# Late modulation sums along rows, with transposed weights, and two steps of a projection group moved to the end of the chunk before

## What is computed

```python
def _modulation(cond, w_mod, b_mod):
    m = jax.nn.silu(cond) @ w_mod + b_mod
    return jnp.split(m, 3, axis=-1)          # shift, scale, gain

sh, sc, g = _modulation(c, w_mod[l], b_mod[l])           # latent tokens
shc, scc, gc = _modulation(c_ctx, w_mod[l], b_mod[l])    # context tokens
h = x * (1.0 + sc) + sh
q, k, v, z = jnp.split(h @ w_in[l], 4, axis=-1)
y = mixer(q, k, v)      # layer 0: neighbourhood attention, layer 1: differential attention
out = (y * jax.nn.silu(z)) @ w_out[l]
x = _layer_norm(DEEPNORM_ALPHA * x + (1.0 + g) * out, ln_g[l], ln_b[l])
```

## Time and profile before

| | |
|---|---|
| median of 3 runs | 1850.34 us (1850.16 to 1850.41) |
| profiled execution | 1850.39 us, span 1848.6 us |
| first layer, chunks 0 to 7 | about 64 to 842 us of the span |
| late loads | 64 DMAs of 256 KB, 2.7 us to landing in the median |
| granted clock of PE | 0.999 of full |

### The profile page before, as it was taken

How to read it: one execution, slowest core, us unless ns; L and a number is a source line. 1 busy time by engine, 2 the same in 40 slices (tenths; PEclk the granted TensorE clock), 3 DMA queues, 4 the chain that set the end, 5 groups by cost and what they waited for, 6 DMA issues and landing times. The chain is left out here.

```text
span 1848.6 us, 30835 instructions
## 1 busy us (share of the span) xinstructions
PE 1802.8 (98%) x10621; PEld 1554.1 (84%) x10621; DVE 1291.5 (70%) x2061; ACT 928.0 (50%) x1680; POOL 269.4 (15%) x219
## 2 busy tenths in 40 slices
PE   7999999999999999989999999999999999999998
PEld 3888888888888888878878889888888888898886
DVE  6677777778687877765868485675848484757658
ACT  2555555555555555560046555464736464554500
POOL 3100000000000000255431010101000010102951
PEclk9999999999999999999999999999999999999999
DMA  9512121312122222225420010101010100101343
GB/s 348 135 47 83 47 82 47 84 38 79 54 74 60 74 60 62 73 94 187 159 80 24 12 45 11 45 0 45 11 45 11 34 23 11 45 11 45 99 143 125
DMA packets 82111, 127.28 MB, mean 69 GB/s; under 512 B 49760, under 2 KB 49920, under 8 KB 81936
## 3 DMA queue, kind: packets, MB, share of 16 engines
q1 hardware_dynamic: 76048, 108.54, 18.7%
q0 software_dynamic: 2384, 8.39, 1.6%
q10 hardware_dynamic: 3632, 9.73, 1.3%
HBM read 108.90 MB, written 20.09 MB: 70 GB/s over the span
## 5 line engine op out<-in xcount | busy, mean ns | idle before, releaser
L548 PE MATMUL acc<-h_hi,w_hi 128*128 128x512 f32 (+1 forms) x1408 | 524.9, 373 | 3.1 <-DVE h_lo L473 1.6
L548 PE MATMUL acc<-h_hi,w_lo 128*128 128x512 f32 (+1 forms) x1408 | 508.7, 361 | 0.0
L548 PE MATMUL acc<-h_lo,w_hi 128*128 128x512 f32 (+1 forms) x1408 | 507.9, 361 | 0.0
L548 PEld LDWEIGHTS acc<-h_hi,w_lo 128*128 128x128 f32 x1408 | 265.3, 188 | 41.5
L548 PEld LDWEIGHTS acc<-h_hi,w_hi 128*128 128x128 f32 x1408 | 265.8, 189 | 40.3 <-DVE h_lo L473 4.7
L548 PEld LDWEIGHTS acc<-h_lo,w_hi 128*128 128x128 f32 x1408 | 266.3, 189 | 33.9
L1676 DVE TENSOR_REDUCE stats<-acc 128x1 f32<-128x1280 f32 x128 | 189.7, 1487 | 43.3 <-PE acc L1775 42.7
L1586 ACT ACTIVATE far_prob<-acc,stats 128x1280 f32<-128x1280 f32 x128 | 170.2, 1330 | 28.3 <-DVE stats L1676 26.5
L1593 ACT ACTIVATE far_pt<-acc 128x512 f32<-128x512 f32 (+1 forms) x192 | 101.1, 527 | 162.0 <-PE acc L1784 158.6
L1775 PE MATMUL acc<-k_dup,q_stack 128*128 128x512 f32 (+1 forms) x768 | 176.7, 367 | 1.8 <-ACT far_prob L1586 0.4
L1797 PE MATMUL acc<-far_pt,far_v 128*128 128x128 f32 x1280 | 172.7, 275 | 0.0
(11 more groups left out here) (208 smaller groups left out, 2906.8 us busy)
## 6 DMA issues: line engine op xcount, KB each, us to landing
w_raw<-in_w_in SPq DMA_DIRECT2D x64, 512.0 KB, 3.3
near_late_slots<-in_w_mod SPq DMA_DIRECT2D x64, 256.0 KB, 2.7
w_raw<-in_w_out SPq DMA_DIRECT2D x16, 512.0 KB, 3.2
w_raw<-y_t POOLq DMA_DIRECT2D x14, 448.0 KB, 5.0
y_t<-y SPq DMA_DIRECT2D x7, 640.0 KB, 3.1
modulation_rows<-in_w_scale SPq DMA_DIRECT2D x8, 512.0 KB, 6.9
modulation_rows<-in_w_mod SPq DMA_DIRECT2D x8, 512.0 KB, 6.7
out_rows<-in_x SPq DMA_DIRECT2D x8, 512.0 KB, 4.5
```

The source lines that it names most:

```text
L548: mm = nc.tensor.matmul(m.bank(self.bank_of(j, c), w), wt[:, b % 2, k, :], ht[:, k, t0:t0 + w], start=(k == 0 and i == 0), stop=(k == KT - ...
```

## The change

The late weights are transposed on the host (`w_late`), so that output columns are the partitions, and the sum over the 1024 inputs goes along a row: in two halves of 512, times four blocks of 128 columns, which are again eight loads of 128 x 512 (u = 4 x half + block). `sum` becomes, for each condition, one `tensor_tensor_reduce` of the slot with a row of coefficients (the condition, the same in all partitions), which writes one number per partition; the second half starts from the first half's number. `reduce` becomes `turn`, one transpose of the 128 x 8 sums. The unused product goes to a free probability buffer, to the slot itself, or, for u > 4, to the other slot; so loads 6 and 7, and the next chunk's load 0, wait for one sum more. The condition is turned at the start and stored in DRAM (`store_cond`); `load_coef` loads 512 of its columns, both conditions, to all partitions, once per half.

Places: SP issues load 6 no longer ahead of `load_next(6)` but behind the bias tables, together with load 7; `load_coef` of the second half stands ahead of load 5, that of the next chunk's first half behind the next chunk's load 1. In the last chunk loads 6 and 7 go behind `out_w.load` 2 and 4, sum 5 to the projections, sums 6 and 7 to DVE's steps 3 and 4, and the products of loads 6 and 7 go. The row is stored by two DMAs of 4 x 128.

Two of eight steps k of the next chunk's group 4 (`BEGUN = 2`) go from the projections to step 10, ahead of `turn`; for chunk 0 they go ahead of the loop. In the last chunk the output projection's pieces (4, 6) and (6, 7) become (4, 5), (5, 6) and (6, 7), the last in step 10.

```diff
+    def store_cond(self, sp):
+        sp.wait_ge(self.act, 2)
+        sp.dma_start(self.cond_rows.rearrange("c (k p) -> (c k) p", p=P), self.cond_buf).then_inc(self.cond_stored, 16)
+
+    def take_cond(self, act):
+        act.wait_ge(self.coef_ready, 1)
+        self.nc.scalar.activation(self.cond_buf, self.m.psum[0:2 * KT, 0, 0:P], ACT.Copy).then_inc(self.act, 1)
...
+        nc.tensor.transpose(m.psum[0:2 * KT, 0, 0:P], m.cond_act[:, :, :].rearrange("p c k -> p (c k)"), m.ident[:, :])\
+            .then_inc(self.coef_ready, 1)
...
     def load(self, sp, c, u):
         if u >= 2:
-            sp.wait_ge(self.summed, CREDIT + c * 2 * KT + 2 * (u - 1))
-        k = u % KT
-        src = self.w_mod[k * P:(k + 1) * P, bass.ds(c * 512 + (D + u // KT * 512), 512)]
-        sp.dma_start(self.slots[k % 2], src).then_inc(self.loaded[k % 2], 16)
+            sp.wait_ge(self.summed, CREDIT + c * 2 * KT + 2 * (u if 5 < u <= KT else u - 1))
+        half = u % KT // 4
+        src = self.w_late[bass.ds(c * 512 + (u // KT * 512 + u % 4 * P), P), half * 512:(half + 1) * 512]
+        sp.dma_start(self.slots[u % 2], src).then_inc(self.loaded[u % 2], 16)
+
+    def load_coef(self, sp, c, half):
+
+        sp.wait_ge(self.summed, CREDIT + c * 2 * KT + KT * half)
+        first = self.cond_rows[0, half % 2 * 512:half % 2 * 512 + 1]
+        src = bass.AP(first.tensor, first.offset, [[0, P], [D, 2], [1, 512]])
+        sp.dma_start(self.coef, src).then_inc(self.coef_loaded, 16)
 
     def sum(self, v, c, u):
+
+        half, t = u // 4, u % 4
         v.wait_ge(self.loaded[u % 2], CREDIT + c * 8 * KT + 16 * (u // 2 + 1))
+        if t == 0:
+            v.wait_ge(self.coef_loaded, CREDIT + c * 32 + 16 * (half + 1))
         if u == 0:
-            v.wait_ge(self.reduced, CREDIT + c * 1)
+            v.wait_ge(self.turned, CREDIT + c * 1)
+        v.wait_ge(self.summed, CREDIT + c * 2 * KT + 2 * u)
+        x = self.slots[u % 2]
         for cnd in range(2):
-            x, coef = self.slots[u % 2], self.m.cond_act[:, cnd, u:u + 1]
-            if u == 0:
-                ins = self.nc.vector.tensor_scalar(self.acc[cnd], x, coef, None, ALU.mult)
-            else:
-                if cnd == 0:
-                    v.wait_ge(self.summed, CREDIT + c * 2 * KT + 2 * u)
-                ins = self.nc.vector.scalar_tensor_tensor(self.acc[cnd], x, coef, self.acc[cnd], ALU.mult, ALU.add)
-            ins.then_inc(self.summed, 1)
-
-    def reduce(self, pe, c, bank):
+            col = cnd * 4 + t
+            unused = x if cnd else self.slots[1 - u % 2] if u > 4 else self.unused[u % 2]
+            self.nc.vector.tensor_tensor_reduce(out=unused, in0=x, in1=self.coef[:, cnd, :], scale=0.5,
+                                                scalar=self.sums[:, 0, col:col + 1] if half else 0.0, op0=ALU.mult, op1=ALU.add,
+                                                accum_out=self.sums[:, half, col:col + 1]).then_inc(self.summed, 1)
+
+    def turn(self, pe, c, bank):
 
         pe.wait_ge(self.summed, CREDIT + c * 2 * KT + 2 * KT)
-        for cnd in range(2):
-            mm = self.nc.tensor.matmul(self.m.psum[0:2, bank, :], self.m.pick[:, cnd, :], self.acc[cnd],
-                                       start=(cnd == 0), stop=(cnd == 1))
-        mm.then_inc(self.reduced, 1)
-
-    def reduce_last(self, pe, c, bank):
-
-        for u in (KT - 2, KT - 1):
-            pe.wait_ge(self.loaded[u % 2], CREDIT + c * 8 * KT + 16 * (u // 2 + 1))
-            self.nc.tensor.matmul(self.m.psum[0:2, bank, :], self.m.cond_act[:, :, u], self.slots[u % 2],
-                                  start=(u == KT - 2), stop=False)
-        pe.wait_ge(self.summed, CREDIT + c * 2 * KT + 2 * (KT - 2))
-        for cnd in range(2):
-            mm = self.nc.tensor.matmul(self.m.psum[0:2, bank, :], self.m.pick[:, cnd, :], self.acc[cnd],
-                                       start=False, stop=(cnd == 1))
-        mm.then_inc(self.reduced, 1)
+        self.nc.tensor.transpose(self.m.psum[0:8, bank, 0:P], self.sums[:, 1, :], self.m.ident[:, :]).then_inc(self.turned, 1)
 
     def take_row(self, act, c, bank):
-        act.wait_ge(self.row_stored, CREDIT + c * 16)
-        act.wait_ge(self.reduced, CREDIT + c * 1 + 1)
-        self.nc.scalar.activation(self.row, self.m.psum[0:2, bank, :], ACT.Copy, scale=0.5).then_inc(self.row_ready, 1)
+        act.wait_ge(self.row_stored, CREDIT + c * 32)
+        act.wait_ge(self.turned, CREDIT + c * 1 + 1)
+        self.nc.scalar.activation(self.row, self.m.psum[0:8, bank, 0:P], ACT.Copy).then_inc(self.row_ready, 1)
 
     def store_row(self, sp, c):
         sp.wait_ge(self.row_ready, CREDIT + c * 1 + 1)
-        sp.dma_start(self.mod_rows[:, bass.ds(c * 512 + ROW_PAD, 512)], self.row).then_inc(self.row_stored, 16)
+        for cnd in range(2):
+            sp.dma_start(self.mod_rows[cnd, bass.ds(c * 4 + ROW_PAD // P, 4), :], self.row[4 * cnd:4 * cnd + 4, :]).then_inc(self.row_stored, 16)
...
-        self.product(pe, c, 4)
+        self.product_part(pe, c, 4, self.BEGUN, KT)
...
-        if not last:
+        if last:
+            late.sum(v, c, 5)
+        else:
             self.split_lo_part(v, self.nc.vector, c, 4)
...
+    fill[NU, MIDDLE] = (1, 4, 0, p.BEGUN)
     filled = {step: piece[0:2] for (step, half), piece in fill.items() if piece[3] == KT}
-    fill_last = {(5, MIDDLE): (0, 2), (7, MIDDLE): (2, 4), (9, MIDDLE): (4, 6), (9, END): (6, 7)}
+    fill_last = {(5, MIDDLE): (0, 2), (7, MIDDLE): (2, 4), (9, MIDDLE): (4, 5), (9, END): (5, 6), (NU, MIDDLE): (6, 7)}
...
-                    for u in (3, 4, 5, 6):
+                    for u in (3, 4):
                         late.load(sp, c, u)
+                    late.load_coef(sp, c, 1)
+                    late.load(sp, c, 5)
                     if last:
                         for k in range(KT):
                             out_w.load(sp, p, k)
-                            if k == 3:
-                                late.load(sp, c, 7)
+                            if k in (2, 4):
+                                late.load(sp, c, 6 if k == 2 else 7)
                     else:
                         p.load_next(sp, c, (6,))
                         biases[1].wait(sp)
...
-                        for u in (7, KT, KT + 1):
+                        for u in (6, 7, KT, KT + 1):
                             late.load(sp, c, u)
+                        late.load_coef(sp, c, 2)
                     late.store_row(sp, c)
...
+                modulation.store_cond(sp)
                 load_first(sp)
...
+                modulation.take_cond(act)
                 p.split_hi_part(act, 0, 0)
...
-                        if col == 0:
-                            act.wait_ge(late.row_stored, CREDIT + c * 16)
...
-                        if step == 3 and last:
-                            late.sum(v, c, 5)
+                        if last and step in (3, 4):
+                            late.sum(v, c, step + 3)
...
+                p.product_part(pe, 0, 4, 0, p.BEGUN)
...
-                                late.reduce_last(pe, c, 1)
-                            else:
-                                late.reduce(pe, c, 7)
+                            late.turn(pe, c, 1 if last else 7)
...
+    w_late = a(np.concatenate([w_mod[0, :, 2 * D:], w_mod[1]], axis=1).T)
```

More of the change, by code:

```diff
@@ L237, in activate @@
         act.wait_ge(self.small_in, 48)
-        self.nc.scalar.activation(self.m.cond_act[:, :, :], self.m.cond[:, :, :], ACT.Tanh, scale=0.5).then_inc(self.tanh_done, 1)
+        self.nc.scalar.activation(self.m.cond_act[:, :, :], self.m.cond[:, :, :], ACT.Tanh, scale=0.5).then_inc(self.act, 1)
     def exp_lambda(self, act):
         act.wait_ge(self.dve, 2)
-        self.nc.scalar.activation(self.sums[:, 2:4], self.sums[:, 0:2], ACT.Exp).then_inc(self.lam_exp, 1)
+        self.nc.scalar.activation(self.sums[:, 2:4], self.sums[:, 0:2], ACT.Exp).then_inc(self.act, 1)
     def take_rows(self, act):
@@ L255, in scale_part @@
         nc.vector.memset(m.mean_mat[:, :], 1.0 / P)
-        for r in range(2):
-            nc.vector.memset(m.pick[:, r, r:r + 1], 1.0)
-            nc.vector.memset(m.pick[:, r, 1 - r:2 - r], 0.0)
         for t in range(KT):
@@ L368, with __init__ @@
     AHEAD = 2
-    def __init__(self, nc, m, near, stack, w_mod, mod_rows):
-        self.nc, self.m, self.w_mod, self.mod_rows = nc, m, w_mod, mod_rows
+    def __init__(self, nc, m, near, stack, w_late, cond_rows, mod_rows):
+        self.nc, self.m, self.w_late, self.cond_rows, self.mod_rows = nc, m, w_late, cond_rows, mod_rows
         sem = lambda n: stack.enter_context(nc.semaphore("x_" + n))
         self.slots = [near.late_slots[:, i, :] for i in range(2)]
-        self.acc = [near.late_acc[:, i, :] for i in range(2)]
-        self.row = near.late_row
+        self.coef, self.row, self.sums = near.late_coef, near.late_row, near.late_sums
+        self.unused = [near.prob[:, 2 + i, 0:512] for i in range(2)]
@@ L597 @@
```

(5 more changed lines are left out.)

53 lines of the change are left out of this document (30 added, 23 removed).

## The result

| | kernel before | changed kernel |
|---|---|---|
| median | 1850.25 us (1850.14 to 1850.41, 4 runs) | 1873.02 us (1871.45 to 1873.70, 4 runs) |
| profiled execution | 1850.39 us, span 1848.6 us | 1873.32 us, span 1871.4 us |
| PE's granted clock, mean | 0.999 | 0.990 (0.990 to 0.992 in the four runs) |

The change costs 1.2%: the ratio is 1.0121, with a 95% interval of 1.0108 to 1.0133. The direction is the predicted one, but the time lies 13 us above the forecast of 1859.6 and outside its range.

A forecast was written before the change was run, and what follows sets the result against it. TensorE (PE), 98% busy, was taken as the bound. 7 x (1.00 + 0.3) per loop chunk, -0.3 for the last chunk and +0.4 at the start gave +9.2 us: 1859.6 us, range 1853 to 1867.

The forecast's parts named there:

- Part 1: End of a loop chunk, seven times: reduce passes out, six matmuls and a transpose in; -0.30 and -1.36, together -1.66 us per chunk.
- Part 2: Load 6 issued later in seven loop chunks: DVE waits 2.85 us ahead of sum 6, PE 2.66 us (bounds 2.2 to 3.0).
- part 4: Second half of the coefficients, eight times: broadcast lands after 4.5 us, gate_silu starts 1.7 us late, mostly covered; +0.3 us per chunk.
- Part 3: The row sums themselves on DVE: 512 columns last 0.71 us, as in the old form; no difference (bounds 0.6 and 1.28).
- rival C: Slower by more: row sums last 1.28 us each, +17 us, giving 1877 us; chance 6%.
- Rival D: Slower by more: coefficient broadcast lands after 5.5 us, 7 x 1.0 us more and 0.5 in the last chunk, 1867 us; 13%.
- Part 5: Last chunk -0.3 us (reduce gone -2.0, sum 7 +1.3, sum 5 and coefficients +0.4); start +0.4 us for one more DMA.
- Rival A: Faster: load 6 is landed when DVE wants it in the loop chunks; 1841.0 us; chance 8%.
- B: Near equal: DVE waits for load 6, but PE only some 1.5 us; 1851.5 us; chance 10%.

## Why the prediction was wrong

**Part 1, right.** The last values start 455.97 - 453.96 = 2.01 us behind the turn, forecast 2.03; without the moved matmuls, where the chain shows alone, it is 2.01 too. The six moved matmuls are worth 1.36 us per chunk (the kernel without them), the transpose in place of the reduce the rest, 0.2 (forecast 0.30). The period with load 6 early is 1.56 below that of before; forecast 1.66.

**Part 2, right in mechanism and size, but priced as a wait only.** DVE's seven waits ahead of sum 6 are 2.75 to 2.99 us in six chunks and 3.67 in the first (forecast 2.85). PE's are 2.35 to 2.59, and 3.28 in the first, 18.0 us together (forecast 7 x 2.66 = 18.6). Without the half clock the seventh copy is 10.6 us later than before (744.07 - 733.50); the prediction's terms up to there, 0.4 + 7 x 2.66 - 7 x 0.30 - 6 x 1.36 + 7 x 0.3, give 10.9. In part that is luck: the waits cost 744.07 - 724.56 = 19.5 us, 0.9 more than forecast, and part 4 was too high by more than that. **The step that failed** is what was left out of this sum: PE's work behind each wait was put down at its old duration, "PE waits 2.66 us", and then as before. In four of seven chunks it took some 1.5 us more at half clock, 6.0 us in all. The rows for this weren't in the trace of before: PE never stood that long in its loop, and behind its stand of 1.59 us in the last chunk the clock stayed at full.

**Part 3, right.** The row sums last 0.69 us (with a constant to start from) and 0.75 (with a pointer), forecast 0.71; rival C, 1.28 us, falls. So does the halved throughput of the Trainium skill (Vector Engine (DVE) Microarchitecture Reference, "Points that are easy to get wrong"), which the prediction cited: with two fp32 sources in SBUF 512 columns take 0.69 us, as long as 512 columns with one source in PSUM (`near_pt_lo<-acc,near_pt_hi`). C's time, 1877 us, came near by accident.

**Part 4, a term too large.** The second coefficients land after 4.7 us (forecast 4.5) and DVE stands 2.7 to 3.2 us for them, as worked out, but PE is late by no more than 0.1 us per chunk, not 0.3: the cover, PE's own stretch up to `scores(1)`, is longer than read. This made the forecast some 1.5 us too high. Rival D falls.

**Part 5, wrong by 7.9 us.** Start +0.4: the size is met (0.41 us in the first copy with load 6 early), but not for the reason given. PE takes up the token rows at 32.70 us, not later than before (32.73); the first 512-column matmul of the weights is then at 60.07 instead of 59.72. What makes these 0.35 us between isn't known. The gains of the last chunk were about right, 3.7 us with sums 6 and 7 out against 3.4. **The step that failed** is "+1.3" for the moved sums in steps 3 and 4: it took their duration from the loop, where GpSimd has nothing to do, and used it where GpSimd splits the output weights. They cost 9.9 us: 2.1 us more for each of the two held row sums, 0.64 for load 6, which was taken as landed, some 1.4 that they cost clear of GpSimd, and a rest of 3.7, put down to the clock behind PE's stands, which no run measures by itself. The kernel before had one row that should have warned, an old sum of 2.09 us in the last chunk; the prediction read only the mean.

Together: 10.6 to the end of the loop (forecast 10.9), 6.0 for the clock in the loop, and 6.2 in the last chunk (forecast -1.7) are 22.8 us. **Rival A** was the change that should have been made: with load 6 landed in time 1841.0 us was forecast, 1845.2 measured with the last chunk's collision left in, and 1838.4 without it. B's condition, a short wait of PE, didn't arise.

## What to carry over

A wait put on the bounding engine is priced with what follows it: where PE would stand in a loop in which it never stood, the work behind the stand may run at half clock, and 2.6 us became 3.4 on average here (24.0 / 7). Where PE would then have waited for another engine anyway, as behind step 3 of the last chunk, the half clock costs nearly nothing and filling the stand gains nearly nothing. A load's place in SP's queue is worth more than the instructions saved: before a buffer is reused, look at what the next load into it is then queued behind, for a scratch of 1 KB per partition turned this change from +22.8 us into -5.5. And an instruction moved to another stage takes its duration from rows of that stage, with the largest beside the mean.

## What was not expected of the hardware

- **The granted clock after a stand.** PE's clock went to its half level for about 3.3 us behind 4 of 7 stands of 2.3 to 3.3 us (changed kernel), 3 of 7 in the same loop (last sums left out) and 4 of 7 (kernel before with load 6 late); behind none of 7 stands of 1.2 us in the loop without the moved quarter, but behind stands of 1.08 and 1.10 us at the start of the loop in two executions, and behind stands of 1.6 to 1.8 us in some executions only. The longer stand isn't the surer one: 3.25 us left it at full. What decides between equal stands is open; nothing here tells it. Filling the loop's stands with matmuls that nobody reads kept it at full. The Trainium skill (TensorE: Matmul & The Clock Gate, "HAM oscillation — how this bites in real kernels") describes a like pattern, work that begins cold after each DMA wait; here it came at waits for DVE, in part of the chunks, and in the changed kernel only 0.5 to 1.5 us into the work.
- **GpSimd holds DVE.** A row sum of 0.75 us with both sources in SBUF that starts within GpSimd's tensor operation ends 0.54 to 0.56 us behind that one (2.85 us beside 2.49, 1.75 beside 1.37), and is not merely slowed.
- **A broadcast landed later than distinct rows.** 512 KB of coefficients, the same for all partitions, took 4.7 us in the median (3.6 to 6.4), where the earlier trace rows have 3.3 us for as many distinct bytes. No run changes the source alone, so it isn't shown that the broadcast makes the difference and not the transfers beside it.
